# Reordering the head of each layer and one tap of the feed-forward convolution in a two-layer streaming encoder

## What is computed

```
for i in range(DEPTH):                       # DEPTH = 2
    xn = rmsnorm(x, norm1_g)                 # x * rsqrt(mean(x*x) + 1e-5) * g
    proj = xn @ w_in                         # q, k, v, sc_b, sc_c, sc_h, cf_a, cf_gate, gate_pre
    glu = cf_a * sigmoid(cf_gate)
    cf_conv = causal_dwconv(glu, hist, cf_conv_w)          # 31 taps, per channel
    ...                                      # attention, short convolution, gates, output projection w_o
    h = rmsnorm(x, norm2_g) @ w_up           # 2 x 2816 columns
    h = causal_dwconv(h, hist, ffn_conv_w)   # 3 taps, per channel
    hg, hu = split(h, 2)
    x = x + (silu(hg) * hu) @ w_down
```

## Time and profile before

| | |
|---|---|
| median of 3 runs | 2416.82 us (2415.88 to 2428.15) |
| profiled execution | 2417.04 us |
| its span, first to last instruction | 2415.8 us |
| PE busy | 2371.0 us, 98% of the span |
| DVE, ACT, POOL busy | 1593.6, 837.0, 113.2 us |
| mean granted clock of PE | 0.992 |

### The profile page before, as it was taken

The page is one execution under the profiler, slowest core; times in us unless marked ns, Lnnn a source line. Parts: engine busy times, 40 slices in busy tenths (PEclk is TensorE's granted clock), DMA queues, the critical chain, the costliest instruction groups (busy, mean ns, idle before and its releaser), DMA issues.

```text
span 2415.8 us, 46512 instructions
## 1 busy us (share of the span) xinstructions
PE 2371.0 (98%) x18142; PEld 2320.5 (96%) x18142; DVE 1593.6 (66%) x2334; ACT 837.0 (35%) x1581; POOL 113.2 (5%) x157
## 2 busy tenths in 40 slices
PE   7999999999999999999999999999999999999997
PEld 6997899999999999999999969999999999999997
DVE  7887788866435664645788878888654456556365
ACT  5126322224423432423432272222253244234243
POOL 0023200000000000000000240000000000000000
PEclk9999999999999999999999999999999999999998
DMA  4221222222232222222232202222223322222222
GB/s 184 83 87 34 70 78 79 80 80 82 93 104 84 79 79 79 85 80 79 89 124 79 89 20 87 79 80 86 79 79 99 104 78 83 78 87 79 79 82 108
DMA packets 57373, 204.31 MB, mean 85 GB/s; under 512 B 8142, under 2 KB 8238, under 8 KB 57006
## 3 DMA queue, kind: packets, MB, share of 16 engines
q1 hardware_dynamic: 52560, 190.03, 22.8%
q0 software_dynamic: 4704, 12.79, 1.8%
HBM read 193.14 MB, written 8.50 MB: 83 GB/s over the span
## 4 chain that ended last, share of the span: by engine, by line
PE 92%; ACT 3%; DVE 3%; issue 1%; DMA 0%; POOL 0%; DVEq 0%; SPq 0%; ACTq 0%; POOLq 0%
PE ps L487 86%; PE ps L516 4%; ACT scratch L910 1%; DVE w_lo L1070 1%; PE ps L618 1%; ACT w_hi L786 1%; PE ps L584 1%; PE ps L602 0%; DVE xn_lo L1173 0%; DMA raw<-in_weights 0%; DVE scratch L1169 0%; PE ps L545 0%; DVE x_q_merged L1559 0%; DVE scratch L1084 0%; ACT branch_hi L930 0%
## 5 line engine op out<-in xcount | busy, mean ns | idle before, releaser
L786 ACT ACTIVATE w_hi<-raw 128x1024 fp32r<-128x1024 f32 x348 | 368.9, 1060 | 1213.7 <-PE ps L487 1160.5
L487 PE MATMUL ps<-xn_hi,w_hi 128*128 128x296 f32 (+1 forms) x3584 | 779.3, 299 | 1.6 <-DVE w_lo L1070 1.6
L487 PE MATMUL ps<-xn_hi,w_lo 128*128 128x296 f32 (+1 forms) x3584 | 778.8, 299 | 0.0
L487 PE MATMUL ps<-xn_lo,w_hi 128*128 128x296 f32 (+1 forms) x3584 | 774.3, 297 | 0.0
L1070 DVE TENSOR_TENSOR w_lo<-raw,w_hi 128x1024 fp32r<-128x1024 f32 x350 | 428.6, 1224 | 488.5 <-ACT w_hi L786 487.0
L487 PEld LDWEIGHTS ps<-xn_hi,w_hi 128*128 128x128 f32 x3584 | 583.0, 189 | 3.7 <-DVE w_lo L1070 1.8
L487 PEld LDWEIGHTS ps<-xn_lo,w_hi 128*128 128x128 f32 x3584 | 582.9, 189 | 0.0
L487 PEld LDWEIGHTS ps<-xn_hi,w_lo 128*128 128x128 f32 x3584 | 579.8, 189 | 0.0
L487 PE MATMUL ps<-branch_hi,w_hi 128*128 128x296 f32 (+1 forms) x1296 | 282.7, 299 | 0.4
L487 PE MATMUL ps<-branch_hi,w_lo 128*128 128x296 f32 (+1 forms) x1296 | 281.6, 299 | 0.0
L487 PE MATMUL ps<-branch_lo,w_hi 128*128 128x296 f32 (+1 forms) x1296 | 279.9, 297 | 0.0
(11 more groups left out here) (166 smaller groups left out, 2023.2 us busy)
## 6 DMA issues: line engine op xcount, KB each, us to landing
raw<-in_weights SPq DMA_DIRECT2D x350, 512.0 KB, 3.4
spill<-x_q_merged POOLq DMA_DIRECT2D x2, 2368.0 KB, 9.3
x_q_merged<-spill POOLq DMA_DIRECT2D x16, 296.0 KB, 3.1
x_q_merged<-in_xt SPq DMA_DIRECT2D x4, 592.0 KB, 8.4
out_y<-x_q_merged SPq DMA_DIRECT2D x8, 296.0 KB, 2.3
scratch<-scratch POOLq DMA_DIRECT2D x64, 18.5 KB, 2.8
con<-in_consts SPq DMA_DIRECT2D x1, 592.0 KB, 11.6
vec<-in_vecs SPq DMA_DIRECT2D x1, 576.0 KB, 4.9
```

Source lines behind the costliest of these rows:

```text
L487: last = nc.tensor.matmul(out[:, h, :], a[:, s, wk], b[:, k, t0 + h * n:t0 + (h + 1) * n], start=(k == 0 and j == 0), stop=(k == nk - 1 an ...
L786: nc.scalar.activation(wh[:, s, :], raw[:, s, :], ACT.Copy).then_inc(hi_done, 1)
```

## The change

It moves instructions; the work is the same but for its order. On PE the first pair of panels of each layer now keeps four tiles for the end in place of three (`alone=4`). In layer 0 the sums stand at index 9 and the spreading at index 12 of the list; in layer 1 they stay at 5 and 8. On ACT and DVE the roundings of the weights move ahead; in layer 0 the first stands between the root and the copy. The sigmoid of the first gate goes behind the last `normed_hi`, and the product that it reads is made later on DVE. Of the first nine taps one stands ahead of the next weights, then four, then four. In `conv_product` the last gate tap, and the value's removal from PSUM, come ahead of the weights' low part, and DVE waits for the panel by itself first.

```diff
-        def two_panels(w, outs, nk, r0, r1, free, kwait, last_late, middle=None):
+        def two_panels(w, outs, nk, r0, r1, free, kwait, last_late, middle=None, alone=3):
+            both = nk - alone
             if last_late:
-                order = [(p, k) for p in range(2) for k in range(nk - 3)]
+                order = [(p, k) for p in range(2) for k in range(both)]
             else:
-                order = [(p, k - 2 * p) for k in range(nk - 1) for p in range(2) if 0 <= k - 2 * p < nk - 3]
-            order += [(p, k) for p in range(2) for k in range(nk - 3, nk)]
+                order = [(p, k - 2 * p) for k in range(nk - 1) for p in range(2) if 0 <= k - 2 * p < both]
+            order += [(p, k) for p in range(2) for k in range(both, nk)]
...
-                if u in (5, 8) and middle:
-                    middle[u == 8]()
+                if middle and u in middle:
+                    middle[u]()
...
-            first_pair(l, W + P_CF, A_CF, D_CF, (nx_lo, l * 24), False, HALF, mh, ml, (mean_square1, root1))
+            first_pair(l, W + P_CF, A_CF, D_CF, (nx_lo, l * 24), False, HALF, mh, ml,
+                       {9: mean_square1, 12: root1} if l == 0 else {5: mean_square1, 8: root1}, 4)
...
-            quarter_root(l, S_N1, A_N1, HALF, O_RT)
-
-            for m in range(3):
+            def first_weights():
+                step(W, P_CF, 0)
+            quarter_root(l, S_N1, A_N1, HALF, O_RT, first_weights if l == 0 else None)
+
+            normed_hi(0)
+            normed_hi(1)
+            if l:
+                normed_hi(2)
+                first_weights()
+                normed_hi(3)
+                step(W, P_CF + 1, 1)
+            else:
+                step(W, P_CF + 1, 1)
+                normed_hi(2)
+                normed_hi(3)
+            for m in range(4, KT):
                 normed_hi(m)
-            step(W, P_CF, 0)
-            normed_hi(3)
-            step(W, P_CF + 1, 1)
-            normed_hi(4)
-            normed_hi(5)
             act.wait_ge(a_out, a_ready(l, A_CF))
             nc.scalar.activation(slot(O_SG, TOK, 0), slot(O_QR, TOK, 0), ACT.Sigmoid).then_inc(glu_gate, 1)
-            normed_hi(6)
-            normed_hi(7)
...
-            first_taps(l, 0, 0, TAPS_GLU // 2)
+            first_taps(l, 0, 0, 1)
...
-                first_taps(l, i * 2 + (j - 1), TAPS_GLU // 2, TAPS_GLU)
-                step(W + i * 4, P_CF + 2 * j + 1, 1)
+                if isinstance(i, int):
+                    first_taps(l, 0, 1, 5)
+                    step(W, P_CF + 3, 1)
+                    first_taps(l, 0, 5, TAPS_GLU)
+                else:
+                    first_taps(l, i * 2 + (j - 1), TAPS_GLU // 2, TAPS_GLU)
+                    step(W + i * 4, P_CF + 2 * j + 1, 1)
...
                         tap(l, 1, hg, gc, m)
-                        step(W + i * 4, p0 + 2 * j + 1, 1)
+                        dve.wait_ge(ff_tap, taps_ + 1)
+                        tap(l, 2, hg, gc, m)
+                        dve.wait_ge(panel_done, W + i * 4 + (p0 + 2 * j + 2))
                         for piece in pieces(first(l)):
...
                         last.then_inc(d_out, 1)
-                        dve.wait_ge(ff_tap, taps_ + 1)
-                        tap(l, 2, hg, gc, m)
+                        step(W + i * 4, p0 + 2 * j + 1, 1)
```

More of the change, by code:

```diff
@@ L560, in residual, with first_pair @@
                     panel(l * PANELS + i * 2 + (w + j), j, d_tile(d + j, half(l)), nk, rh, rl)
-        def first_pair(l, w, a, d, kwait, last_late, n, rh, rl, middle=None):
+        def first_pair(l, w, a, d, kwait, last_late, n, rh, rl, middle=None, alone=3):
             two_panels(w, (a_tile(a, n), d_tile(d, n)), KT, (rh, rl), (rh, rl), ((a_out, a_free(l, a)), (d_out, d_free(l, d))),
-                       kwait, last_late, middle)
+                       kwait, last_late, middle, alone)
         def pair(l, w, a, d, rg, ro, n, kwait=None, middle=None):
@@ L768, in _ @@
                 if t0 == 0:
-                    first_pair(l, W + p0, a0, d0, (nx_lo, l * 24 + 16), True, half(l), xh, xl, (mean_square, root2))
+                    first_pair(l, W + p0, a0, d0, (nx_lo, l * 24 + 16), True, half(l), xh, xl, {5: mean_square, 8: root2})
                     up(0, 1)
@@ L809, in root, with quarter_root @@
                 .then_inc(a_out, 1)
-        def quarter_root(l, s, a, n, at):
+        def quarter_root(l, s, a, n, at, between=None):
             nc.scalar.activation(warm[:, :], eps, ACT.Sqrt)
@@ L816, in quarter_root @@
                 .then_inc(rms_done, 1)
+            if between:
+                between()
             act.wait_ge(sum_ps, l * NS + (s + 2))
@@ L1089, in rsqrt, with quarter_rsqrt @@
             dve.wait_ge(rs_done, count)
-        def quarter_rsqrt(a_at, n, count, roots):
+        def quarter_rsqrt(a_at, n, count, roots, between=None):
             dve.wait_ge(rms_done, roots)
             V.reciprocal(rms[:, 0:n // 2], rms[:, 0:n // 2]).then_inc(rs_done, 1)
+            if between:
+                between()
             dve.wait_ge(a_out, a_at)
@@ L1174, in normed_lo, with first_weights @@
                                        ALU.subtract).then_inc(nx_lo, 1)
-            quarter_rsqrt(a_ready(l, A_N1), HALF, l * 3 + 1, l * 2 + 1)
+            def first_weights():
+                step(W, P_CF, 0)
+            quarter_rsqrt(a_ready(l, A_N1), HALF, l * 3 + 1, l * 2 + 1, first_weights if l == 0 else None)
             normed(0)
@@ L1181, in _ @@
             normed_lo(1)
-            step(W, P_CF, 0)
             normed(3)
-            normed_lo(2)
-            V.tensor_tensor(halves(slot(O_QR, TOK, 0)), halves(view(O_RT, TOK)), a_tile(A_CF), ALU.mult).then_inc(a_out, 1)
+            if l:
+                first_weights()
+                normed_lo(2)
+                step(W, P_CF + 1, 1)
+            else:
+                normed_lo(2)
+                step(W, P_CF + 1, 1)
             normed(4)
             normed_lo(3)
[L1188 to L1192, removed]
+            normed(5)
+            normed_lo(4)
+            V.tensor_tensor(halves(slot(O_QR, TOK, 0)), halves(view(O_RT, TOK)), a_tile(A_CF), ALU.mult).then_inc(a_out, 1)
+            normed(6)
+            normed_lo(5)
+            normed(7)
+            normed_lo(6)
+            normed_lo(7)
             V.memset(G[:, :, 0:CF_H], 0.0).then_inc(g_zero, 1)
```

## The result

The changed kernel took 2406.72 us, the median of seven executions (2399.25 to 2411.01), against 2416.82 (2414.35 to 2428.15) before. The ratio is 0.9947, with a 95% interval of 0.9926 to 0.9968: faster by about half a per cent, and the interval doesn't reach 1. The forecast was 2405.2, just short of that half per cent. The single times are more telling than the median: of the kernel before, six of seven lie between 2414.4 and 2418.2; of the changed one, two are near 2399.7, three near 2406 and two near 2411. The profiled execution is one of the longest, with a span of 2409.7, only 6.1 less than before.

A forecast was written before the change was run, and what follows sets the result against it. PE, busy for 98% of the span, was taken as the bound, so its waits were priced: 4.5 + 3.3 + 2.0 + 2.0 = 11.8 us off 2417.04 gives 2405.2, range 2402.0 to 2409.5.

The forecast's parts named there:

- Layer 0's head: Layer 0's first panels: panel 4 starts at 44.3, 6.2 sooner; after a new wait at panel 6, 4.5 us are left.
- a new wait ahead of panel 6: Layer 0: three taps now behind panel 4's low part delay panel 6's, so PE waits about 1.7 us.
- the start: Layer 0's opening: nine units on PE end at 20.2, as DVE's squares come; the idle 3.1 and low clock go.
- DVE's chain: Layer 0's head: DVE sets the pace from first normed at 25.4 to panel 4's low part at 43.0.
- Layer 1's head: Layer 1's first panels: panel 4 starts 3.6 us sooner; a wait of 0.2 is left later, so 3.3 us.
- The feed-forward's ends: Last end of each layer's feed-forward: earlier value removal and taps remove both PE waits, 2.0 us per layer.
- the 44 tiles: Feed-forward tiles of both layers: the low part stands behind 1.65 us more work, at no cost, with 1.1 to spare.
- The clock didn't fall at the new wait: Rival: the clock falls behind layer 0's 1.7 us wait at panel 6, costing 1.7 us: 2406.9; chance 0.15.
- The tap stayed long: Rival: the first tap, no longer starting with POOL's memset, saves 0.9 us per layer: 2403.4; chance 0.14.
- The feed-forward's waits went: Rival: the waits at the feed-forward's ends only change releaser, so 4.0 us don't come: 2409.2; chance 0.12.
- no tile was late: Rival: the value's low part is late in the feed-forward's 44 tiles, costing 26 us: 2431; chance 0.05.
- The step that failed: Whole kernel: the terms' 11.8 us are taken from the one profiled execution's 2417.04, giving 2405.2.

The follow-up runs named there:

- the filled pair: The kernel before and the changed kernel, each with eleven unread matmuls in two pauses of PE at each attention's start: 2411.60 and 2399.98 us.
- heads_only: The changed kernel with conv_product as in the kernel before, pauses not filled: 2409.28 us, ratio 0.9976 to the kernel before.
- after_filled: The changed kernel with eleven unread matmuls in the two pauses of PE at each attention's start: 2399.98 us.
- after_filled_again: The changed kernel with the same eleven unread matmuls, run once more as a control: 2399.37 us, ratio 0.9911 to the kernel before.
- before_filled: The kernel before with eleven unread matmuls in the two pauses of PE at each attention's start: 2411.60 us, ratio 0.9977 to it unfilled.
- the next two sets: The changed kernel run again without any edit, twice: 2399.60 us (five executions) and 2409.90 us (ten executions).

## Why the prediction held, and where it didn't

**Layer 0's head: 4.5 forecast, 3.6 measured** (3.55 in the filled pair; in the first two traces the low parts are 4.15 ahead behind this head, of which 0.37 is an earlier first matmul). The mechanism is right: no idle time ahead of the sums, no low clock behind them, panel 4 limited by DVE, a new wait ahead of panel 6 (1.7 forecast, 1.40 measured). The term that was too large in these pairs is the start. The prediction put nine units' end at 20.2, from five units that ended at 16.90, and the sums come at 20.59. Before, the five units had time to spare, and PE's pace in the opening didn't matter; now the sums wait for PE itself. PE's timelines of heads_only and then after_filled show that the pace in the opening is not the same each time:

```profile
13.35 0.57 PE L515 MATMUL ps<-merged_hi,w_lo 128*128 128x296 f32 x2
13.75 0.43 PE L515 MATMUL ps<-merged_hi,w_hi 128*128 128x296 f32 x2
```

```profile
16.19 0.62 PE L515 MATMUL ps<-merged_hi,w_lo 128*128 128x296 f32 x2
16.65 0.43 PE L515 MATMUL ps<-merged_hi,w_hi 128*128 128x296 f32 x2
```

Two matmuls take 0.69 until about 13.4 in the one and 16.2 in the other, 0.43 from there on, so the sums stand at 19.87 or at 20.85. The order of heads_only differs from that of after_filled only later; and after_filled_again, the same kernel as after_filled, changes pace at 14.0 and has its sums at 20.15. There the term is 4.6: panel 20 is 4.26 ahead of that of before_filled (145.93 and 150.19), from a first matmul that is 0.36 later (11.01 and 10.65). The kernel before changed pace at 14.0 as well, and the forecast's 4.5 holds for an opening like that one; with a longer slow start it is 3.6.
The Trainium skill, page "TensorE: Matmul & The Clock Gate", section "Part 1: The HAM clock gate", says that the number of slow matmuls at a kernel's start differs from run to run of the same kernel. The two traces of the filled changed kernel agree, with 16.7 and 14.0.
The rest of the term, DVE's chain, came out as worked: from the first `normed` to the low part of panel 4 17.6 forecast, 43.45 - 26.03 = 17.4 measured.

**Layer 1's head: 3.3 forecast, 3.4 measured** (9.02 - 5.58). **The feed-forward's ends: 2.0 each forecast, 2.0 and 2.0 measured** (5.58 - 3.55 and 10.99 - 8.99). The sum is 11.0 by the table, 11.1 by the spans, 11.6 by the medians of the filled pair, for 11.8 forecast; with the layer 0 term of after_filled_again it is 12.1. Nothing was lost in the 44 tiles.

**The rivals.** The clock didn't fall at the new wait: panel 6 starts behind its 1.40 with two matmuls in 0.54, and the granted clock from 59.49 to 63.49 is 1.00. The tap stayed long in the changed kernel itself. The feed-forward's waits went, and no tile was late.

**The step that failed** is in the sum: "The profiled execution took 2417.04 [...] 2417.04 - 11.8". It takes every other stage of that execution as fixed. The attentions are not: their clock, 0.67 and 0.82 in the two stretches shown of before, was in the trace and was not read, because PE counts as busy there and the prediction looked at waits. A stage at half clock has no wait. Without a fall the changed kernel takes 2399 to 2400, below the lower end of the range (2402.0); with a long one it takes 2405 to 2415. The median of 2406.72 lies 1.5 beside the forecast, but it is a median over both kinds, and the nearness is in part luck: the next two sets gave 2399.60 and 2409.90, both outside the range. At equal clock the sum of the terms stands: 2411.60, of the filled kernel before, less 11.8 is 2399.8, and after_filled took 2399.98.

## What to carry to other kernels

A span that is nearly all PE still has time in it that no wait shows: read the granted clock stage by stage before making a sum against one execution, and hold it fixed in both kernels when comparing them. Here eleven useless matmuls in two pauses of each layer made the kernel before 5 us shorter and made a difference of 11.6 us readable that had hidden in a scatter of 16. When a stall of PE is moved, price it twice, by its length and by the clock behind it: undoing the split of the taps cost 6.4 where its waits come to 3.3. And when a change makes the sums of squares wait for PE itself, the pace of the opening, which differs from run to run, becomes part of what the change is worth.

## What the runs showed of the hardware

The fall in the attention comes at a stretch in which no pause of PE is over 0.96, while a wait of 1.40 at the head was followed by no fall, and waits of 2.02 and 3.34 were. In the attention's start PE works on small tiles (64x16 to 64x144); whether the pauses or these small matmuls bring the fall can't be told from the fill, which closes the pauses with full-sized matmuls. Once fallen, the clock stayed at 0.50 for over 20 us in some executions, with PE recorded as busy for 10.00 of 10.00. And in the opening PE's matmuls take 0.69 for two, not 0.43, while the granted clock of those stretches reads 1.00 (from 10.00 to 16.00 in the changed kernel): the rows of the clock don't show that start.
